# A hybrid attention and state-space block on one core: index weights in two pieces, two index sums earlier, the last products ordered by bank, the last token tile in 512-column pieces

## The reference, cut to what matters

```python
def hybrid_layer(x, positions, g_norm, w_in, ...):          # x: 1 x 512 x 2048
    h = rms_norm(x, g_norm)
    proj = h @ w_in
    q, k, v, att_gate, q_idx, k_idx, w_idx, u, ssm_gate, merge = jnp.split(proj, offsets, axis=-1)
    # q, k, q_idx (16 heads of 64), k_idx (one head of 64): partial rotary
    w_idx = w_idx * (IDX_HEADS ** -0.5)
    att = dsa_attention(q, k, v, q_idx, k_idx, w_idx)
    y_a = (att * jax.nn.silu(att_gate)) @ w_att_out
    s = jax.nn.gelu(s5_ssm(u, ...))
    s = s * jax.nn.sigmoid(s @ w_glu + b_glu)
    y_b = (s * jax.nn.silu(ssm_gate)) @ w_ssm_out
    gates = jax.nn.sigmoid(merge + b_merge).reshape(bsz, l, N_BRANCH, D_MODEL)
    mixed = gates[:, :, 0] * y_a + gates[:, :, 1] * y_b
    return x + mixed @ w_out

# in dsa_attention, for each block of 128 queries:
    logits = jnp.einsum("bqhd,bsd->bqhs", qi_blk, k_idx) * (IDX_DIM ** -0.5)
    score = jnp.einsum("bqhs,bqh->bqs", jax.nn.relu(logits), w_blk)
    # the 128 keys with the highest score are attended to

# and at the end
    return rms_norm(x, g_final)
```

## Time and profile before

| | us |
|---|---|
| runs of the kernel before: median (lowest to highest, 3 runs) | 1141.2 (1140.92 to 1142.79) |
| the profiled execution: its own time | 1142.43 |
| the profiled execution: span from first to last instruction | 1140.6 |
| TensorE busy | 1126.0 |
| VectorE busy | 753.3 |
| ScalarE busy | 433.2 |

### The profile page before, as it was taken

How to read it: one execution, slowest core, us unless ns; L and a number is a source line. 1 busy time by engine, 2 the same in 40 slices (tenths; PEclk the granted TensorE clock), 3 DMA queues, 4 the chain that set the end, 5 groups by cost and what they waited for, 6 DMA issues and landing times.

```text
span 1140.6 us, 13391 instructions
## 1 busy us (share of the span) xinstructions
PE 1126.0 (99%) x5326; PEld 927.9 (81%) x5326; DVE 753.3 (66%) x1267; ACT 433.2 (38%) x574; POOL 49.0 (4%) x54
## 2 busy tenths in 40 slices
PE   8999999999999999999999999999999999999997
PEld 5998888888888788888777777788888888788885
DVE  6788579998466548347788887354144454877485
ACT  7722333433344443332122313333412232654374
POOL 1000000014100000000000000000000000000000
PEclk9999999999999999999999999999999999999999
DMA  9433343457432146754445564454466231577755
GB/s 366 187 122 136 116 143 111 111 141 154 149 111 75 37 131 161 145 134 134 126 164 142 128 158 120 129 171 147 112 157 156 93 111 48 196 265 256 242 191 203
DMA packets 57166, 170.53 MB, mean 150 GB/s; under 512 B 10912, under 2 KB 21312, under 8 KB 47632
## 3 DMA queue, kind: packets, MB, share of 16 engines
q1 hardware_dynamic: 35968, 133.84, 34.6%
q0 software_dynamic: 13040, 33.93, 14.0%
q10 hardware_dynamic: 8096, 1.91, 0.8%
HBM read 163.37 MB, written 37.75 MB: 176 GB/s over the span
## 4 chain that ended last, share of the span: by engine, by line
PE 92%; DVE 5%; ACT 1%; DMA 1%; issue 0%; SPq 0%; DVEq 0%; ACTq 0%
PE banks L575 24%; PE banks L577 23%; PE banks L576 23%; PE banks L824 4%; PE banks L826 4%; PE banks L825 4%; PE banks L731 2%; PE banks L712 2%; DVE w_lo L1302 1%; PE banks L721 1%; PE banks L781 1%; PE banks L679 1%; PE banks L680 1%; PE banks L797 1%; DVE par L1485 1%; DMA x_fm<-in_x_fm 1%
## 5 line engine op out<-in xcount | busy, mean ns | idle before, releaser
L575 PE MATMUL banks<-act_hi,w_hi 128*128 128x512 f32 (+1 forms) x1088 | 421.7, 388 | 0.5 <-DVE w_lo L1302 0.5
L577 PE MATMUL banks<-act_hi,w_lo 128*128 128x512 f32 (+1 forms) x1088 | 416.8, 383 | 0.0
L576 PE MATMUL banks<-act_lo,w_hi 128*128 128x512 f32 (+1 forms) x1088 | 416.7, 383 | 0.0
L575 PEld LDWEIGHTS banks<-act_hi,w_hi 128*128 128x128 f32 x1088 | 204.4, 188 | 39.6 <-issue 3.9
L577 PEld LDWEIGHTS banks<-act_hi,w_lo 128*128 128x128 f32 x1088 | 204.2, 188 | 38.4
L1302 DVE TENSOR_TENSOR w_lo<-w_raw,w_hi 128x2048 fp32r<-128x2048 f32 x78 | 178.5, 2289 | 84.8 <-ACT w_hi L926 84.0
L576 PEld LDWEIGHTS banks<-act_lo,w_hi 128*128 128x128 f32 x1088 | 204.5, 188 | 35.1 <-issue 0.2
L926 ACT ACTIVATE w_hi<-w_raw 128x2048 fp32r<-128x2048 f32 (+1 forms) x81 | 154.2, 1904 | 150.8 <-DMA w_raw<-in_w_tiles 148.1
L1789 DVE TENSOR_TENSOR w_lo<-w_raw,w_hi 128x512 fp32r<-128x512 f32 (+1 forms) x64 | 67.6, 1088 | 34.0 <-ACT w_hi L1204 33.8
L1204 ACT ACTIVATE w_hi<-w_raw 128x512 fp32r<-128x512 f32 (+1 forms) x64 | 59.4, 948 | 60.7 <-DMA w_raw<-w_sums 39.8
L1187 ACT ACTIVATE gate<-gate,g_cols 128x512 f32<-128x512 f32 x16 | 11.6, 723 | 129.4 <-DVE gate L1751 129.4
(11 more groups left out here) (318 smaller groups left out, 1468.3 us busy)
## 6 DMA issues: line engine op xcount, KB each, us to landing
w_raw<-in_w_tiles SPq DMA_DIRECT2D x67, 1024.0 KB, 4.9
w_sums<-in_w_out POOLq DMA_DIRECT2D x24, 1024.0 KB, 8.4
w_raw<-w_sums SPq DMA_DIRECT2D x32, 512.0 KB, 4.5
w_sums<-w_sums POOLq DMA_DIRECT2D x8, 1024.0 KB, 11.1
w_raw<-in_w_att_out SPq DMA_DIRECT2D x8, 1024.0 KB, 5.4
w_raw<-in_w_out SPq DMA_DIRECT2D x16, 512.0 KB, 4.6
x_tok<-in_x SPq DMA_DIRECT2D x4, 1024.0 KB, 12.7
w_raw<-in_w_ssm_out SPq DMA_DIRECT2D x4, 1024.0 KB, 5.1
```

What stands on the lines that cost most here:

```text
L575: nc.tensor.matmul(out_ap, wh, x_hi[k], start=(j == 0), stop=False)
L576: nc.tensor.matmul(out_ap, wh, x_lo[k], start=False, stop=False)
L577: last = nc.tensor.matmul(out_ap, wl, x_hi[k], start=False, stop=(j == n - 1))
```

## The change

Five edits. (1) w_key is loaded in two transfers: the first four slices ahead of x, the other twelve behind the second chunk of x; ACT rounds the first piece before it waits for the parameters, and the second piece ahead of slice 4 of x. (2) DVE adds the first two indexer items ahead of its rotation of the eighth tile of index queries. (3) For the last two slices of the third run, in both halves, the products are ordered tb, part, k, so that each bank's six passes stand together. (4) For the last two token tiles ACT squares 512 columns at a time, each as soon as its bank is added; the first sum is scaled and carried over as a bias of the root by one more small instruction. (5) The last token tile is scaled and stored in four pieces of 512 columns.

The whole diff, without lines of context:

```diff
@@ -80,0 +81 @@
+EARLY_ITEMS = 2
@@ -81,0 +83 @@
+KEY_FIRST = 4
@@ -304,0 +307 @@
+        key_raw, key_high = sem("key_raw"), sem("key_high")
@@ -386 +389 @@
-            return count + 14 * HALF_K - 8 + 3 * tb + 2 * (k - HALF_K + 2) + part
+            return count + 14 * HALF_K - 8 + 3 * tb + 2 * part + k - HALF_K + 2
@@ -427 +430,2 @@
-            sp.dma_start(w_raw[:, 0, 0:KD * n0].rearrange("p (k n) -> p k n", k=KD), w_key).then_inc(raw_loaded[0], 16)
+            key = w_raw[:, 0, 0:KD * n0].rearrange("p (k n) -> p k n", k=KD)
+            sp.dma_start(key[:, 0:KEY_FIRST, :], w_key[:, 0:KEY_FIRST, :]).then_inc(key_raw, 16)
@@ -429,0 +434,2 @@
+                if c == 1:
+                    sp.dma_start(key[:, KEY_FIRST:KD, :], w_key[:, KEY_FIRST:KD, :]).then_inc(raw_loaded[0], 16)
@@ -506 +512 @@
-            for i, t in enumerate(LAST_TOKENS):
+            for i, t in enumerate(LAST_TOKENS[0:3]):
@@ -511 +517,6 @@
-            sp.wait_ge(stored, 2 * 16 * TOK)
+            t = LAST_TOKENS[3]
+            for c in range(2):
+                for finished, col in ((final_done, c * 512), (final_rest_done, HALF + c * 512)):
+                    sp.wait_ge(finished, 4 + c)
+                    sp.dma_start(out_v[t][:, col:col + 512], res[:, t, col:col + 512]).then_inc(stored, 16)
+            sp.wait_ge(stored, 2 * 16 * TOK + 2 * 16)
@@ -629 +640 @@
-            pe.wait_ge(high_done, 1)
+            pe.wait_ge(key_high, 1)
@@ -631,0 +643,2 @@
+                if k == KEY_FIRST:
+                    pe.wait_ge(high_done, 1)
@@ -901,3 +914,3 @@
-                    for k in (HALF_K - 2, HALF_K - 1):
-                        wait_quarter(n0 + k, 0)
-                        for part in range(2):
+                    for part in range(2):
+                        for k in (HALF_K - 2, HALF_K - 1):
+                            wait_quarter(n0 + k, 0)
@@ -924 +937 @@
-                    n_el = KD * (IDX_DIM + IDX_HEADS) if u == 0 else UNIT
+                    here = slice(KEY_FIRST * (IDX_DIM + IDX_HEADS), KD * (IDX_DIM + IDX_HEADS)) if u == 0 else slice(0, UNIT)
@@ -926 +939 @@
-                    nc.scalar.activation(w_hi[:, u % SLOTS, 0:n_el], w_raw[:, u % SLOTS, 0:n_el], ACT.Copy).then_inc(high_done, 1)
+                    nc.scalar.activation(w_hi[:, u % SLOTS, here], w_raw[:, u % SLOTS, here], ACT.Copy).then_inc(high_done, 1)
@@ -938,0 +952,3 @@
+            key_n = KEY_FIRST * (IDX_DIM + IDX_HEADS)
+            act.wait_ge(key_raw, 16)
+            nc.scalar.activation(w_hi[:, 0, 0:key_n], w_raw[:, 0, 0:key_n], ACT.Copy).then_inc(key_high, 1)
@@ -940 +955,0 @@
-            high_through(0)
@@ -941,0 +957,2 @@
+                if first == KEY_FIRST:
+                    high_through(0)
@@ -1248,0 +1266,11 @@
+            def root_of_parts(i):
+                t = LAST_TOKENS[i]
+                act.wait_ge(part_ready, 2 * i - 1)
+                link(nc.scalar.activation(square_out[:, 0, :], res[:, t, HALF:HALF + 512], ACT.Square, accum_out=small[:, 176 + t:177 + t]))
+                link(nc.scalar.activation(square_out[:, 2, 0:1], small[:, 176 + t:177 + t], ACT.Identity, bias=small[:, 180 + t:181 + t],
+                                          scale=1.0 / D))
+                act.wait_ge(part_ready, 2 * i)
+                link(nc.scalar.activation(square_out[:, 1, :], res[:, t, HALF + 512:D], ACT.Square, accum_out=small[:, 176 + t:177 + t]))
+                nc.scalar.activation(small[:, 184 + t:185 + t], small[:, 176 + t:177 + t], ACT.Sqrt, bias=square_out[:, 2, 0:1],
+                                     scale=1.0 / D).then_inc(squares_done, 1)
+
@@ -1278,3 +1306,8 @@
-            for i in (2, 3):
-                root_of(i)
-                scale_half(i)
+            root_of_parts(2)
+            scale_half(2)
+            root_of_parts(3)
+            act.wait_ge(scale_ready, 4)
+            for c in range(2):
+                here = slice(c * 512, c * 512 + 512)
+                nc.scalar.activation(res[:, LAST_TOKENS[3], here], res[:, LAST_TOKENS[3], here], ACT.Copy,
+                                     scale=small[:, 188 + LAST_TOKENS[3]:189 + LAST_TOKENS[3]]).then_inc(final_done, 1)
@@ -1337,0 +1371 @@
+                    dve.wait_ge(key_high, 1)
@@ -1399,0 +1434,14 @@
+            start = {1: 0, 2: 2 * P, 3: 5 * P}
+            scores = {b: score[:, start[b]:start[b] + (b + 1) * P] for b in start}
+
+            def add_item(n):
+                b, h = 1 + n // IDX_HEADS, n % IDX_HEADS
+                dve.wait_ge(relu_done, n + 1)
+                r, w = relu[:, n % 2, 0:(b + 1) * P], w_idx[:, b, h:h + 1]
+                if h == 0:
+                    ins = v.tensor_scalar(scores[b], r, w, None, ALU.mult)
+                else:
+                    ins = v.scalar_tensor_tensor(scores[b], r, w, scores[b], ALU.mult, ALU.add)
+                ins.then_inc(acc_done, 1)
+                dve.wait_ge(acc_done, n + 1)
+
@@ -1400,0 +1449,4 @@
+                if i == 7:
+                    dve.wait_ge(wv_ready, 1)
+                    for n in range(EARLY_ITEMS):
+                        add_item(n)
@@ -1418,17 +1469,0 @@
-            start = {1: 0, 2: 2 * P, 3: 5 * P}
-            scores = {b: score[:, start[b]:start[b] + (b + 1) * P] for b in start}
-            dve.wait_ge(wv_ready, 1)
-
-            def add_item(n):
-                b, h = 1 + n // IDX_HEADS, n % IDX_HEADS
-                dve.wait_ge(relu_done, n + 1)
-                r, w = relu[:, n % 2, 0:(b + 1) * P], w_idx[:, b, h:h + 1]
-                if h == 0:
-                    ins = v.tensor_scalar(scores[b], r, w, None, ALU.mult)
-                else:
-                    ins = v.scalar_tensor_tensor(scores[b], r, w, scores[b], ALU.mult, ALU.add)
-                ins.then_inc(acc_done, 1)
-                dve.wait_ge(acc_done, n + 1)
-
-
-
@@ -1450 +1485,2 @@
-                    add_item(n)
+                    if n >= EARLY_ITEMS:
+                        add_item(n)
@@ -1869,3 +1905 @@
-                part = add_part(tb, half * HALF, a_banks[tb])
-                if half == 0:
-                    part.then_inc(bank_taken, 1)
+                add_part(tb, half * HALF, a_banks[tb]).then_inc(part_ready if half else bank_taken, 1)
@@ -1915 +1949,6 @@
-            finish(3)
+            dve.wait_ge(scale_ready, 4)
+            t = LAST_TOKENS[3]
+            for c in range(2):
+                here = slice(HALF + c * 512, HALF + c * 512 + 512)
+                v.scalar_tensor_tensor(res[:, t, here], res[:, t, here], small[:, 188 + t:189 + t], g_last[:, here], ALU.mult, ALU.mult
+                                       ).then_inc(final_rest_done, 1)
```

## The result

The changed kernel takes 1143.43 us (median of 20 executions, 1142.04 to 1144.84); the kernel before, beside it on the same chip, 1141.8 (20 executions, 1140.77 to 1142.79). The ratio is 1.0016, 95% interval [1.0009, 1.0022]: slower by 1.6 us, where 2.0 us less were forecast. The execution profiled took 1142.99 us, 0.56 more than that of before. In each of the two profiles TensorE's start has one stretch at the lower clock, so the difference between them does not hold all of the difference between the medians. The mean granted clock of the profiled execution is 0.997; 16 of the 20 executions of the change have 0.994 or 0.995, so the profile shown is one of the better ones.

What follows compares the result with a forecast made beforehand. TensorE, busy 1126.0 of 1140.6 us, was taken as the bound, so gains lie only where it stands still. -1.78 + 0.25 + 0.0 - 0.5 = -2.0 us gave a median of 1139.2 from 1141.2, range 1137.3 to 1141.0.

Steps and rivals of the forecast that it cites:

- Sums ahead of the eighth rotation (-1.8): Indexer at 105 us: TensorE's wait at item 4's logits goes whole, with no new stall; -1.8 us.
- The key weights in two pieces (+0.25): Start: slices 2 and 4 arrive as before, a later second rounding delays TensorE's dense run; +0.25 us, between 0 and +0.5.
- The clock (0, ±1.3): TensorE's start: one low-clock stretch stays as it was, 0; its loss or repetition would make ±1.3 us.
- The step from the Trainium skill: TensorE's clock: the point of change isn't tied to kernel start, so before and after have the same spread; no size.
- Products by bank, squares (0.0): Last two token tiles: first inverse earlier, but ScalarE's own chain replaces the wait for the add; 0.0 us.
- a bound of 0.2: Last token tile's inverse: order by bank and squares could gain at most 0.2 us or cost 0.2.
- The last tile in four pieces (-0.5): Last stores: first issued 0.5 us earlier, and the end of the stores follows it; -0.5 us.
- the bound of +0.2: Last stores in four pieces: the worse bound, if the end hangs on the last issue; +0.2 us.
- The estimate of 4 us for fixed parts that do not overlap: Last stores: with no overlap of fixed DMA cost, four pieces would be some 4 us slower than two; not used.
- The second: Start: a second slow-clock stretch, as the pause in front of slice 2 grows; -0.7, 1140.5 us; chance 0.08.
- the third: Last stores gain nothing, as smaller pieces move slower or the last issue decides; -1.4 to -1.5, 1139.7 us; chance 0.10.
- The fifth: Last stores: fixed parts of small pieces do not overlap, so slower than before; +2.4, 1143.6 us; chance 0.03.

Runs made afterwards that it cites:

- i3_change_two_stores: Whole change with nine short unused products in TensorE's pauses, but the last tile's two stores of before; 1141.46 us, ratio 0.9999 to the kernel before.
- h1_change_fill: Whole change plus nine short unused products in TensorE's pauses at the start, nothing else; 1142.22 us, ratio 1.0003 to the kernel before.
- g1_fill_order_sq: Kernel before with early sums, four short products, last products ordered by bank and squares by 512 columns; last tile still in two stores; 1139.69 us.
- i1_front_all_fill: Whole change, but both key-weight pieces sent ahead of x, plus short products in TensorE's pauses; 1140.19 us, ratio 0.9988 to the kernel before.
- h2_front_fill: Kernel before with early sums, short products and key weights in two pieces, both ahead of x; tail as before; 1139.69 us, ratio 0.9982.
- e3_tail: Kernel before with only the end's edits: products by bank, squares by 512 columns, four last stores; 1141.85 us, ratio 1.0006.
- the first four runs: Kernel before with early sums, split key weights or tail edits alone, and the change without its key edit; 1140.22, 1144.13, 1141.85, 1139.67 us.
- the groups f and h: Two sets of runs varying the key pieces' place and short products, each with its own executions of the kernel before: 1141.43 and 1141.68 us.
- the base: Kernel before with the two early index sums and four short unused products in TensorE's pauses at the start; 1139.54 us, 1139.61 when run again.
- f3_split_fill: Kernel before with only the key weights in two pieces as in the change, plus nine short products in TensorE's pauses; 1145.39 us, ratio 1.0032.

## Why the prediction was wrong, by its steps

Forecast was 1139.2 and measured 1143.43. Of the 4.2 us between them, 0.6 are the starting point: the three executions shown had a median of 1141.2, the twenty beside the change one of 1141.8. The other 3.6 are the sum's, +1.6 instead of -2.0. The medians of kernels that differ by one thing account for it (by nearly one: `i3_change_two_stores` and `h1_change_fill` have nine short products, the others four). From `g1_fill_order_sq` to `i3_change_two_stores` (late slices): 1139.69 to 1141.46, +1.8. From there to `h1_change_fill` (four stores on top of the key edit): +0.8; `i1_front_all_fill` against `h2_front_fill` gives +0.5 for the same. From there to the change (no short products, so the clock): +1.2; without the key edit the same products are worth 1140.22 less 1139.54, 0.7, so the key edit's own part of the clock is +0.5. With the early sums' -0.9 to -1.4 this makes +1.4 to +2.2; measured are +1.6. These medians stand on chips and executions that differ by some tenths: by the ratios to before the slices are +1.4, the end +0.5 to +0.7, the clock +1.5. Each is a difference of two ratios that are known to 1 us or so. That the late slices cost is clear: all executions of `i3_change_two_stores` (1140.75 to 1143.23) lie above all of `g1_fill_order_sq` (1139.45 to 1140.21). How large each term is, is known only roughly, and of the longer end's +0.5 to +0.8 only the profiles are sure.

**Sums ahead of the eighth rotation (-1.8).** Right in the mechanism: no wait at an item, none at item 5, first sum ahead of the rotation, VectorE's low part at 109.52 less the 1.75 of the late start, 107.8, for 107.9 forecast. Alone it brought 0.9 to 1.4. Where TensorE's start runs at full clock the pause is shorter in the first place (1.50 us in `e3_tail`), and pauses of 0.3 to 0.7 us behind VectorE's low parts come up at 30 to 40 us: TensorE was going to wait for VectorE somewhere. That this is all of the missing 0.4 to 0.9 is not shown.

**The key weights in two pieces (+0.25).** This is the step that failed. It is the largest error: with +1.8 in its place the sum is -0.5 instead of -2.0, and with the +0.5 of clock that the edit brings too it is 0; the rest up to +1.6 are what the sums did not bring and the stores. It said that slice 2 and slice 4 arrive as before, since "in front of either the same bytes are sent", and put the extra issue down as free. The second rounding was right (0.99 us, between slices 3 and 4), and so was what it does: VectorE's low part starts at 12.49 instead of 10.45, 2.04 later, which is 1.79 for the slices and the forecast 0.25. But the slices came at 10.16 and 12.66. Equal bytes ahead did not mean equal landing: 2.67 MB had been moved when slice 2 could be used, before 2.22. It is +1.8 where +0.25 was forecast.

**The clock (0, ±1.3).** Its place and size were right, the choice was not. I wrote that the pause in front of slice 2 grows and left that to a rival of 0.08. In the change 16 of 20 executions had a mean granted clock of 0.994 or 0.995, of before one of 142 beside the experiments; at 0.997 or more were 3 of 20 of the change and 111 of 142 of before (28 of 29 beside the first four runs, but 16 of 26 and 16 of 27 beside the groups f and h). The step from the Trainium skill (TensorE: Matmul & The Clock Gate, on what is actually happening) that the point of change varies from run to run agrees with the spread of single kernels; that before and after would therefore have the same spread does not. The kernel before had less of it, and its one profile, with a slow stretch and a clock of 0.996, was of an execution of the minority.

**Products by bank, squares (0.0).** Right: tile 0's inverse 0.42 us ahead of the last pass for 0.5 forecast (that it stands at 1131.56 where 1131.6 was written is chance, since the forecast was in the times of before), the last inverse 2.98 after the last pass instead of 2.82 with a bound of 0.2; 0.1 us in time.

**The last tile in four pieces (-0.5).** Wrong; the outcome lies at the other end, near the bound of +0.2. The first store is only 0.28 us sooner, the four issues take 1.80 us, 0.45 each and not 0.37, so the last quarter is issued 5.3 us after the last pass and lands 2.9 us later; what the first store gains, the last one gives back: +0.0 to +0.1 on the base. The estimate of 4 us for fixed parts that do not overlap did not come either. The rest, +0.5 to +0.8 in company of the key edit, was in no case of mine.

**The rivals.** The second (a longer slow stretch) took part, the third (stores gain nothing) was right as far as it went. The fifth names 1143.6, close to what was measured, but its mechanism is refuted: no pause between the stores, and four stores on the base cost nothing. That its number fits is chance. I priced a slower outcome at 0.04 because I had looked for it at the end and at the items, not in the transfer that the key edit puts between the x chunks.

## What to carry to other kernels

In a start that waits for transfers, put what is needed first in front as one block, and don't squeeze a piece between the chunks that the engines wait for: measure when each chunk lands, and don't reckon it from the bytes ahead alone. Where small waits remain at TensorE, the clock they may cost can be larger than they are, so a change that lengthens a pause in the start needs several executions' clocks, of both kernels, before its price is set; a few short products in the pauses took 0.7 to 1.2 us off here by the medians. And edits that were free one by one need not be so together: with the key edit and the four stores in one program an instruction packet stood in the middle of the last stores, and the end was 0.6 to 0.7 us longer in each of the three profiles.

## What the runs showed that I had not expected

- With a piece of 480 KB between the x chunks the 16 DMA engines moved 246 GB/s from 3 to 5 us instead of 378, and the chunk behind it was usable 1.8 us later with the same bytes in front of it; by then 0.45 MB more of later chunks had been moved.
- A pause of TensorE of 2.1 us in the middle of a dense run was followed by 3.6 us at a mean clock of 0.59, which cost some 1.5 us (`f3_split_fill`).
- The last stores' end came 0.6 to 0.7 us later with a single 8 KB instruction packet among them (9.22, 9.38 and 9.31 us from last pass to end, against 8.6 to 8.7).
